# Moving taps of two depthwise filters from TensorE and VectorE to ScalarE and GpSimd, with nine small edits to waits and orders

## The reference, cut to what matters

```
mix : h = rmsnorm(x);  z = h @ w_in                     # 1024 -> 2560: a_h, a_bg, a_cg, b_val, b_gate, 512 each
      y_a = a_bg * dwconv(a_cg * a_h, conv_a_w)         # branch a: 3 taps per channel
      u   = dwconv(b_val * sigmoid(b_gate), conv_b_w) + conv_b_b      # the long filter: 31 taps per channel
      y_b = silu(layernorm(u));  x += concat(y_a, y_b) @ w_out
ffn : h = rmsnorm(x);  x += (silu(dwconv(h @ w_gate)) * (h @ w_up)) @ w_down
ret : two rmsnorms, four heads of retention, x += y @ w_out
mlp0: x += relu(h @ w1)**2 @ w2
att : 16 heads of banded chunk attention with a relative bias
mlp1: as mlp0, with other weights;  then out = rmsnorm(x)
```

## Time and profile before

| | us |
|---|---|
| median of 3 runs (1954.25 to 1959.22) | 1954.38 |
| the profiled execution's own time | 1950.77 |
| its span in the trace | 1949.0 |
| TensorE busy in it | 1895.9 (97%) |
| VectorE, ScalarE, GpSimd busy | 1084.2, 680.3, 792.2 |

### The profile page before, as it was taken

The page is one execution under the profiler, slowest core; times in us unless marked ns, Lnnn a source line. Parts: engine busy times, 40 slices in busy tenths (PEclk is TensorE's granted clock), DMA queues, the critical chain, the costliest instruction groups (busy, mean ns, idle before and its releaser), DMA issues.

```text
span 1949.0 us, 22390 instructions
## 1 busy us (share of the span) xinstructions
PE 1895.9 (97%) x8716; PEld 1570.3 (81%) x8716; DVE 1084.2 (56%) x1471; ACT 680.3 (35%) x976; POOL 792.2 (41%) x325
## 2 busy tenths in 40 slices
PE   7998999999999999999999999999999999999997
PEld 5776888888878888888888888888888888888886
DVE  5887872662685534343572616265877674435263
ACT  4224432222363333232442222233666542222232
POOL 4332444444454333343344444444233344444441
PEclk9999999999999999999999999999999999999998
DMA  5212332442232222222233232323433223232321
GB/s 173 92 65 65 119 102 93 138 142 94 86 103 74 78 87 87 87 87 86 65 117 98 92 104 89 105 86 98 112 107 102 76 87 103 92 98 96 96 99 44
DMA packets 163239, 186.31 MB, mean 96 GB/s; under 512 B 3760, under 2 KB 143296, under 8 KB 163024
## 3 DMA queue, kind: packets, MB, share of 16 engines
q1 hardware_dynamic: 154512, 169.36, 27.0%
q10 hardware_dynamic: 8640, 15.75, 3.0%
HBM read 178.76 MB, written 6.33 MB: 95 GB/s over the span
## 4 chain that ended last, share of the span: by engine, by line
PE 80%; DVE 8%; issue 7%; ACT 2%; POOL 2%; DMA 0%; ACTq 0%; DVEq 0%; POOLq 0%; SPq 0%
PE ps L394 26%; PE ps L396 26%; PE ps L395 26%; POOL w_lo L383 2%; DVE sum_of_squares L1177 1%; DVE xl L1161 1%; ACT w_hi L776 1%; DVE hid_lo L1235 1%; PE ps L682 1%; DMA x<-in_x_dram 0%; DVE x L1215 0%; PE ps L489 0%; ACT hid_hi L789 0%; PE ps L664 0%; PE ps L474 0%
## 5 line engine op out<-in xcount | busy, mean ns | idle before, releaser
L383 POOL TENSOR_TENSOR w_lo<-raw,w_hi 128x1024 fp32r<-128x1024 f32 x320 | 791.8, 2478 | 1122.9 <-ACT w_hi L776 1122.9
L776 ACT ACTIVATE w_hi<-raw 128x1024 fp32r<-128x1024 f32 x320 | 336.4, 1058 | 748.6 <-PE ps L396 747.2
L394 PE MATMUL ps<-xh,w_hi 128*128 128x512 f32 x1408 | 556.4, 395 | 16.2 <-DVE xl L1161 15.2
L396 PE MATMUL ps<-xh,w_lo 128*128 128x512 f32 x1408 | 549.3, 390 | 0.0
L395 PE MATMUL ps<-xl,w_hi 128*128 128x512 f32 x1408 | 549.2, 390 | 0.0
L394 PE MATMUL ps<-hid_hi,w_hi 128*128 128x512 f32 x944 | 370.1, 392 | 10.5 <-issue 7.4
L395 PE MATMUL ps<-hid_lo,w_hi 128*128 128x512 f32 x944 | 368.1, 390 | 0.0
L396 PE MATMUL ps<-hid_hi,w_lo 128*128 128x512 f32 x944 | 367.9, 390 | 0.0
L394 PEld LDWEIGHTS ps<-xh,w_hi 128*128 128x128 f32 x1408 | 265.1, 188 | 74.9 <-issue 14.2
L395 PEld LDWEIGHTS ps<-xl,w_hi 128*128 128x128 f32 x1408 | 265.2, 188 | 56.1 <-issue 2.4
L396 PEld LDWEIGHTS ps<-xh,w_lo 128*128 128x128 f32 x1408 | 265.0, 188 | 55.8
(11 more groups left out here) (179 smaller groups left out, 1558.5 us busy)
## 6 DMA issues: line engine op xcount, KB each, us to landing
raw<-in_mlp_w_dram SPq DMA_DIRECT2D x64, 1024.0 KB, 5.3
raw<-in_ret_w_in_dram SPq DMA_DIRECT2D x24, 1024.0 KB, 5.1
raw<-in_att_w_in_dram SPq DMA_DIRECT2D x12, 1024.0 KB, 5.5
raw<-in_w_gate_dram SPq DMA_DIRECT2D x11, 1024.0 KB, 5.3
raw<-in_w_up_dram SPq DMA_DIRECT2D x11, 1024.0 KB, 5.3
raw<-in_w_in_dram SPq DMA_DIRECT2D x10, 1024.0 KB, 5.3
raw<-in_w_down_dram SPq DMA_DIRECT2D x8, 1024.0 KB, 5.4
raw<-in_ret_w_out_dram SPq DMA_DIRECT2D x8, 1024.0 KB, 5.1
```

Source lines behind the costliest of these rows:

```text
L383: nc.gpsimd.tensor_tensor(view[0], view[1], view[2].bitcast(F32), ALU.subtract).then_inc(w_lo, c.made(w_lo))
L394: nc.tensor.matmul(o, a[0], b[0], start=first, stop=False, skip_group_check=True)
L396: return nc.tensor.matmul(o, a[1], b[0], start=False, stop=last, skip_group_check=True)
L776: nc.scalar.activation(view[0], view[1], ACT.Copy).then_inc(w_hi, c.made(w_hi))
```

## The change

The taps of the second pair go 4 to TensorE (8 products), 5 to ScalarE and GpSimd, 22 to VectorE (before: 11, 0, 20). ScalarE multiplies shifted views by the weights into `filter_pieces` behind units 8 and 9, GpSimd adds them, and VectorE's first tap starts from that sum. Branch a's filter goes likewise: ScalarE scales behind units 13 to 16, GpSimd adds three pieces and multiplies by `r_bc`, with 3 instructions per tile, put behind the low part of the halves 15 to 18. `tap_w` is made one unit earlier.

```diff
-TENSOR_TAPS = 11
+TENSOR_TAPS = 4
+POOL_TAPS = 5
+PARTS_BEHIND = {11: (2, 1, 3), 12: (2, 3, 5), 13: (3, 1, 3), 14: (3, 3, 5)}
+SHORT_BEHIND = {15: 0, 16: 1, 17: 2, 18: 3}
+LONG_BEHIND = {8: 2, 9: 3}
+APAD_BEHIND = {13: 0, 14: 1, 15: 2, 16: 3}
-ADDS_AFTER = {3: (1,), 5: (2,), 7: (3, 4, 5, 6, 7)}
+ADDS_AFTER = {7: (1, 2, 3, 4, 5, 6, 7)}
+WARM_FIRST, WARM_LAST = 9, 4
+OUT_BY_POOL = (6, 7)
 # GpSimd
+            def long_part(t, first, end):
+                for n in range(first, end):
+                    pool.wait_ge(long_scaled, (t - 2) * POOL_TAPS + n + 1)
...
+                    nc.gpsimd.tensor_tensor(cacc[:, t, :], so_far, long_piece[t - 2][n], ALU.add)...
+            def short_filter(t):
+                pool.wait_ge(short_scaled, 3 * t + 3)
...
+                nc.gpsimd.tensor_tensor(y, a, b, ALU.add)...
+                nc.gpsimd.tensor_tensor(y, y, d, ALU.add)...
+                nc.gpsimd.tensor_tensor(y, y, r_bc[:, :], ALU.mult).then_inc(short_ready, ...)
+            for u in range(MIX_UNITS):
+                low_half(u // 2 % 2, u % 2)
+                if u in PARTS_BEHIND: long_part(*PARTS_BEHIND[u])
+                if u in SHORT_BEHIND: short_filter(SHORT_BEHIND[u])
 # TensorE
+            pe.wait_ge(w_landed[0], 16)
+            keep_warm(WARM_FIRST)               # 128x128 products of ones before the first unit
-                    unit8(X)
-                    stats()
+                    unit8(X, between=stats)     # inside unit 2, not behind it
-                    unit4(H, 0, ready=hid_ready, fresh=True)
+                    unit4(H, 0, ready=hid_ready, fresh=2)      # in the mixing stage and in each retention head
-            stats()
-            spread()
+            last_stats()                        # the last square is summed by TensorE, not by VectorE
+            keep_warm(WARM_LAST)
+            spread(ST, r_spread)                # waits for one diagonal at a time
+            spread(0, r_spread, 6)              # a second copy, for GpSimd
 # ScalarE, mixing stage
-                        for g in taps_after(u):
+                        after_unit()
+                        for g in taps_after(u + 1):
...
+                        if u in LONG_BEHIND:    # 5 pieces behind each of units 8 and 9
+                        if u in APAD_BEHIND:    # 3 pieces behind each of units 13 to 16
 # VectorE, mixing stage: conv_step 3, 3, 3, 3 behind units 4 to 7 (before 3, 3, 2, 2), 2 after them,
 # 4 behind units 8 to 11 (before 3) and 12 to 15, then 3, 3, 1 behind 16 to 18
-                        (lines 1336, 1339, 1342: branch a's filter)
+                        dve.wait_ge(short_ready, c.next(short_ready))
                         dve.wait_ge(unit_done, c.next(unit_done))
+                        V.tensor_tensor(short[t], short[t], bank(), ALU.mult)...
```

More of the change, by code:

```diff
@@ L197, in part @@
             return v if len(shape) == 1 else v.rearrange("p (a b) -> p a b", a=shape[0])
-        upad, cacc, apad, gbuf, ybuf = (part(0, 4, UPW), part(2168, 4, SEQ), part(4216, 4, SEQ + 2),
-                                        part(6272, 2, SEQ), part(7296, 2, SEQ))
+        upad, cacc, apad, gbuf = (part(0, 4, UPW), part(2168, 4, SEQ), part(4216, 4, SEQ + 2), part(6272, 2, SEQ))
         r_sq = gbuf[:, 0, :]
+        piece = [pieces[:, SEQ * n:SEQ * (n + 1)] for n in range(2 * POOL_TAPS + 6)]
+        long_piece = [piece[0:POOL_TAPS], piece[POOL_TAPS:2 * POOL_TAPS]]
+        short_piece = [piece[2 * POOL_TAPS:2 * POOL_TAPS + 3], piece[2 * POOL_TAPS + 3:]]
+        short = [part(at, SEQ) for at in (7296, 7808, 6272, 6784)]
         ln_squares = [apad[:, t, 0:SEQ] for t in range(4)]
@@ L375, in _, with low_half @@
             nc.gpsimd.memset(ones[:, :], 1.0).then_inc(ones_set, 1)
+            def low_half(slot, half):
+                pool.wait_ge(w_hi, c.next(w_hi))
+                cut = (slice(None), slot, slice(None), slice(HALF * half, HALF * (half + 1)))
+                view = [t[:, :, :].rearrange("p s (k c) -> p s k c", c=256)[cut] for t in (wl, raw, wh)]
+                nc.gpsimd.tensor_tensor(view[0], view[1], view[2].bitcast(F32), ALU.subtract).then_inc(w_lo, c.made(w_lo))
             def pair(i):
@@ L742, in _ @@
                     pe.wait_ge(mix_ready, ATT_HEADS - 2)
[L743 removed]
+                    unit4(H, 4, fresh=0, last=(mix_ready, ATT_HEADS))
                     for _ in range(3):
@@ L796, in prep @@
                     nc.scalar.activation(xh[:, d, :], x[:, d, :], ACT.Copy, scale=prow(name, row + d)).then_inc(hi_made, c.made(hi_made))
-                nc.scalar.activation(squares[:, 2 * (place % 2), :], x[:, d, :], ACT.Square).then_inc(curve_made, c.made(curve_made))
+                signal = last_square if kind == "final" and place == KT - 1 else curve_made
+                nc.scalar.activation(squares[:, 2 * (place % 2), :], x[:, d, :], ACT.Square).then_inc(signal, c.made(signal))
                 if kind == "norm":
                     return
-                act.wait_ge(curve_made, c.now(curve_made))
+                act.wait_ge(signal, c.now(signal))
                 if kind == "final":
@@ L1110, in _ @@
             make_root()
+            act.wait_ge(hi_made, c.now(hi_made))
+            act.wait_ge(r_spread, 2)
+            nc.scalar.activation(r_bc[:, :], ps[:, 6, :], ACT.Copy).then_inc(r_copied, 1)
+            for done, n in enumerate(OUT_BY_POOL):
+                act.wait_ge(pool_ready, done + 1)
+                act.dma_start(out[P * n:P * (n + 1), :], x[:, n, :]).then_inc(out_stored, 16)
         @block.vector
@@ L1137, in mean_square, with diagonals @@
                 V.tensor_scalar(ms, ps[:, 4, 0:ST], 1.0 / n, eps, ALU.mult, ALU.add).then_inc(to_curve, c.made(to_curve))
-            def diagonals(col, spread=True):
+            def diagonals(col, spread=True, parts=1):
+                if parts > 1:
+                    for i in range(ST):
+                        V.tensor_scalar(diag[:, i, :], ident[:, :], col[:, i:i + 1], None, ALU.mult).then_inc(
+                            stats_in, c.made(stats_in))
+                    dve.wait_ge(r_spread, 1)
+                    return
                 each = bass.AP(ident[:, :].tensor, ident[:, :].offset, [ident[:, :].ap[0], [0, ST], [1, P]])
@@ L1168, in start_sums, with sum_squares @@
                 V.memset(ssq[:, :], 0.0).then_inc(signal, c.made(signal))
-            def next_input(d, place, prepare, signal, last):
-                kind, name, row = prepare
+            def sum_squares(place, prepare, signal, last):
                 def add_squares(total, which, signal):
@@ L1652, in _ @@
                     banks[0] = 4
-                    for n in range(4):
-                        qk_taken(n)
-                        qk_lo(n)
+                    qk_taken(0)
+                    qk_taken(1)
+                    qk_lo(0, 1)
+                    dve.wait_ge(*c.own())
+                    qk_taken(2)
+                    qk_lo(1, 1)
+                    dve.wait_ge(*c.own())
+                    qk_taken(3)
+                    qk_lo(2, 1)
+                    qk_lo(3)
                     banks[0] = 2
```

193 lines of the change are left out of this document (127 added, 66 removed).

## The result

The changed kernel took 1936.73 us (median of 4 runs, 1936.28 to 1937.14), the kernel before 1954.32 us (4 runs, 1951.89 to 1959.22). The ratio is 0.9919, with a 95% interval of 0.9903 to 0.9934. It became faster and stayed within the range, 1.3 us inside its upper end, but the forecast of 1925 is 11.7 us too low. The two profiled executions are 1950.77 and 1937.11 us, 13.7 apart; in that frame, in which the sum was made, 15.6 of the 29.3 us are missing.

A forecast was written before the change was run, and what follows sets the result against it. TensorE, busy 1895.9 of 1949.0 us, was taken as the bound. Terms of 12.3 + 1.75 + 5.6 + 3.2 + 1.2 + 2.2 + 1.0 + 2.0 sum to 29.3 us, so 1921.5 for the execution, 1925 for the median; range 1917 to 1938.

The forecast's parts named there:

- Taps and their weights: Mixing stage: 14 products leave TensorE, 12.3 us; the last taps no longer wait for `tap_w`, 1.75 us.
- The entry into the output product: Mixing stage, unit 20: 7.3 us of wait and slow clock go, less charges of 1.2 and 0.5 us.
- that for `hid_lo`: Unit 20: TensorE still waits 1.2 us for VectorE's third `hid_lo`; 3.5 or none at the bounds.
- The charge for GpSimd's queue: Low part for unit 19, behind GpSimd's additions at 1.2 us each, costs 0.5 us; none at 0.68, 14 at 2.4.
- the 1.7 at which the forecast was to fall: Sign: if GpSimd's 128x512 rows take over 1.7 us, not 1.2, the forecast falls.
- took ScalarE as free: Mixing stage: ScalarE does at most 4.9 us per unit, under the 5.44 between units, so it costs nothing.
- a pause so short doesn't bring the slow clock: Unit 20: a wait of 1.2 us leaves the clock high, as 2.56 us in attention did.
- The two rivals, GpSimd's queue and VectorE: Mixing stage: GpSimd's queue delays `w_lo`, 1930 to 1939 us, chance 0.12; VectorE bounds unit 20, 1932 us, chance 0.12.
- Entries of the stages: `xl` before the squares removes a 0.4 us wait in three stages, 1.2 us; retention 0 (other end 2.6), heads 0.
- The start: Products of ones raise the clock early, 1.8 us; sums, `stats` and diagonals net 1.4; 3.2 us together, bounds 0 to 3.6.
- Attention: First v unit's wait shrinks by 2.2 us, three later waits 0, the fourth 1.0 us.
- The end: Earlier last sums, and scalings and stores shared out: 2.0 us, between 3.3 earlier and 0.6 later.

The follow-up runs named there:

- the light GpSimd: Kernel after with GpSimd's short filter cut to the product alone, two of branch a's three taps left out, so not the reference: 1931.45 us, 0.9891.
- the old orders: Kernel after with ScalarE's and VectorE's orders ahead of the stages as before the change: 1935.52 us, 0.9905.
- the kernel with six taps: Kernel after with six long-filter taps on GpSimd, not five, for the last two tiles, and branch a's filter one half later in its queue: 1931.89 us, 0.9894.

## Why the prediction missed, step by step

**Taps and their weights: right.** 5.44 us between unit ends from unit 13 on, and no wait for `tap_w`. 12.3 + 1.75 us are there.

**The entry into the output product: the first step that failed.** Forecast 5.6 us of gain; 3.7 us of waits and 1.7 of clock leave 1.9 of it in the trace. Of the text's two charges, that for `hid_lo` came out small (1.2 forecast, 0.51 measured), but by luck. VectorE ended the long filter where the working had it: at 137.9 on the old time axis, which is 136.9 here (unit 13 ends at 102.9 there and 101.87 here), and 136.53 was measured. But the third `hid_lo`, due at 138.7, or 137.7 here, was ready at 141.6, and TensorE waited so little for it because it was itself almost 5 us late.

The charge for GpSimd's queue ("So I charge **0.5 us**") was the error: 3.2 us, and the clock as well. GpSimd's instruction was 1.30 us (1.37 with its hand-over), inside the bounds and under the 1.7 at which the forecast was to fall. With it the low part for unit 19 should have been there 1 to 2 us after the T + 26.9 to 27.7 of the working (T is 101.87); it was there at T + 30.6. The Trainium skill, "GPSIMD Engine Reference", section "Elementwise — side-by-side cycle accounting", gave the estimate of 1.12; the measured 1.30 is 16% above, over twelve such instructions 2.2 us. What the working left out is what a late GpSimd holds up besides `w_lo`: the `raw` slot, so SP's load, so ScalarE's conversion and the pieces queued behind it. Of the lateness 1.8 us are this, and about as much is the instruction's own time. It was costed as a queue, and it is a ring through three engines and a DMA. The working also took ScalarE as free, from its busy time; it stood 7.14 and 8.68 us at two conversions, with what GpSimd and VectorE needed behind them. And the remark that a pause so short doesn't bring the slow clock was argued from one row (2.56 us in attention). Here 2.72 us did, and so did 2.55 in attention itself in the kernel with the mixing stage's change alone.

The two rivals, GpSimd's queue and VectorE, were not alternatives but stood in line: behind `w_lo` came `hid_lo`, 2.48 and 3.08 us. Relieving both gave 4.8 us.

The rule of the Trainium skill's page "SBUF — State Buffer", section "SBUF: two separate sides", of VectorE and GpSimd at one port pair holds: the `hid_lo` rows of after are 0.90 to 2.47 us beside GpSimd, and two of those with the light GpSimd are 0.68 and 0.70. The sum of 2.70 us at 180.58 ended 0.6 us after GpSimd's instruction.

**"Entries of the stages", heads included: the largest miss.** Forecast 1.2 us gained; measured 4.6 lost, a swing of 5.8. The step took away a wait for `xl` (0.4) and never asked what is late next. Next is the sum of squares, which frees nothing until it is done and now stands behind `xl` on VectorE: the output product in front of it waits 0.95. The sums were also taken to be the same work in either order, and they are 15 us longer in all, since they meet GpSimd more often. For the heads, that `hid_lo` "already was the last to come" held, but starting earlier exchanged waits of 1.04 to 1.17 for one of 1.40. Retention, "0, with 2.6 as the other end", lost 0.6 in waits. The 1.7 us of low clock in after's profile can't be laid on the edit: with the old orders five of six profiles have a dip there too, behind `stats`. The profile of before is the sixth, and the sum stood on it.

**The start: 3.2 forecast, 0.85 measured.** The products of ones do what they were said to (the x products are 0.23 us apart by 17 us), but what they save only brings TensorE to `stats` earlier, and VectorE's sums, seven in a row now, end at 30.1, not at 28.2. The wait is 1.23, not 0.6, and in five of the eleven profiles with that wait a low clock worth 1.7 us follows it.

**Attention: right in sum, wrong in its parts.** Forecast 2.2 + 0 + 1.0. In the traces 2.23 at the v unit, 0.86 in the three later groups and 0.09 in the fourth, 3.2 in all; the runs say 6.0 for the edit, of which 2.8 aren't explained. That the sum came out near was therefore partly luck: the term for the fourth group was 1.0, and 0.09 stand there.

**The end: 2.0 forecast,** 0.6 in the traces, 0.5 to 1.2 in the runs. The sums' wait shrank from 2.37 to 1.58 and VectorE's scalings by 1.2, but the two tiles that GpSimd scales leave last.

**The sum.** By the traces of before and after: 12.3 + 1.75 + 1.9 + 1.1 (start) - 2.8 (entries) - 2.3 (retention, with its slow products) - 1.2 - 1.3 (heads, and the wait at 654.07, which the change didn't make) + 3.2 + 0.6 = 13.3, against 13.7. The single edits undone on the chip don't add as well: from the kernel after by old start, attention and end (+7.3) and undone orders and heads (-4.5), mixing alone should take 1939.5; it took 1943.6. Four us of interplay stay open; dips of the clock, which come and go between executions, are what I would look at first.

## What to carry to other kernels

When work is put on an engine's queue, follow everything that the engine frees, not only what it makes: the buffer that it reads last decides when the next load starts, and so when the engines in front of it can go on. After each wait removed ask for the next one by name and time; removing `xl`'s 0.4 us in three stages without that lost 2.8 in sum. And where several waits of 1 to 3 us end in the same unit, relieve them together, or each single relief will look as if it were worthless (1.7 us), while both give 4.8.

## What the runs showed of the hardware

TensorE's granted clock fell from 2.4 to 1.2 GHz behind short waits, each time for about six to thirteen products of 128x512, which cost 1.1 to 2.6 us. It did so in some executions of the same kernel and not in others. Behind the wait of 1.2 us for the sums of the start, which stands before the tiny 128x1 products of `stats`, it fell in five of eleven profiles. Behind the 2.7 us for `w_lo` before unit 19 it fell in six of eight, and behind the 2.55 us in attention in one of three. A wait of 3.2 us before retention did it in ten of the eleven profiles that have it; with the old orders there, the clock fell in five of six, but later, behind `stats`. Filling the 3.2 us with products of ones kept the clock there, and it fell 10 us later, behind a wait of 1.18 us.

A VectorE instruction with two operands in SBUF takes 0.68 to 0.70 us for 128x512 with GpSimd idle. Beside GpSimd's it took up to 2.53 us as a `hid_lo` and 2.70 as the sum at 180.58, while eight taps with one operand in PSUM took 5.36 us beside a busy GpSimd and 5.37 before.

In the group with the kernel with six taps, the kernel before scattered by 7.3 us (1950.2 to 1957.5, eight runs) and that with six taps by 0.7 (1931.55 to 1932.28, four runs). Dips of the clock that come and go are the likely reason (argued from the profiles, since the other runs left none), and the profile of before, with 1950.77, was among the better executions.
